# Two attention steps at a time: scores of four units, then values of four units, in every second step

## The reference

```python
s = jnp.einsum('znqhd,znkhd->znhqk', qb, kb) * (Dh ** -0.5)
s = jnp.where(valid[None, :, None], s + bias[None, None], -jnp.inf)
lse = jax.nn.logsumexp(s, axis=-1)
p = jnp.exp(s - lse[..., None])
o = jnp.einsum('znhqk,znkhd->znqhd', p, vb)
```

## Time and profile before

| | |
|---|---|
| median of three runs | 2827.86 us |
| profiled execution, own time | 2828.97 us |
| its span | 2827.2 us |
| TensorE busy | 2801.3 us, 99% |
| VectorE, ScalarE, GpSimd busy | 61%, 47%, 6% |
| granted TensorE clock, mean | 0.996 of 2.4 GHz |
| steps of the first attention (first score matmul to end of its filler) | 59.6 to 391.5 us |

### The profile page before, as it was taken

The page is one execution under the profiler, slowest core; times in us unless marked ns, Lnnn a source line. Parts: engine busy times, 40 slices in busy tenths (PEclk is TensorE's granted clock), DMA queues, the critical chain, the costliest instruction groups (busy, mean ns, idle before and its releaser), DMA issues.

```text
span 2827.2 us, 34929 instructions
## 1 busy us (share of the span) xinstructions
PE 2801.3 (99%) x13264; PEld 2270.1 (80%) x13264; DVE 1726.0 (61%) x2477; ACT 1333.7 (47%) x2149; POOL 180.7 (6%) x133
## 2 busy tenths in 40 slices
PE   8999999999999999999999999999999999999998
PEld 7777777888888888888777788888888888888886
DVE  5333356235866666678666524988235866666786
ACT  5444452114555454445355424887123655544452
POOL 1222420000000000000033200000000000000000
PEclk9999999999999999999999999999999999999998
DMA  3111111123344366532321111211113334384442
GB/s 127 38 31 38 39 38 51 52 62 117 131 149 153 150 236 231 186 109 93 128 61 53 45 54 59 60 54 59 53 60 142 134 149 156 139 322 162 156 134 71
DMA packets 86126, 302.75 MB, mean 107 GB/s; under 512 B 9552, under 2 KB 9680, under 8 KB 79696
## 3 DMA queue, kind: packets, MB, share of 16 engines
q1 hardware_dynamic: 84672, 295.88, 30.7%
q10 hardware_dynamic: 1296, 4.72, 0.6%
HBM read 225.07 MB, written 75.50 MB: 106 GB/s over the span
## 4 chain that ended last, share of the span: by engine, by line
PE 97%; DVE 1%; issue 1%; ACT 0%; DMA 0%; POOLq 0%; POOL 0%; SPq 0%; DVEq 0%; ACTq 0%
PE ps L404 24%; PE ps L2450 17%; PE pa L2756 11%; PE ps L2756 11%; PE ps L2785 9%; PE pa L2785 9%; PE pa L404 4%; PE ps L2803 3%; PE ps L2632 2%; PE pa L2560 2%; PE pa L2528 2%; PE pa L2539 1%; PE pa L2499 1%; PE pa L2632 0%; PE ps L2462 0%
## 5 line engine op out<-in xcount | busy, mean ns | idle before, releaser
L394 DVE TENSOR_TENSOR w_lo<-w_raw,w_hi 128x1024 fp32r<-128x1024 f32 x134 | 160.0, 1194 | 395.0 <-ACT w_hi L388 394.9
L388 ACT ACTIVATE w_hi<-w_raw 128x1024 fp32r<-128x1024 f32 x134 | 137.8, 1029 | 385.2 <-PE ps L404 265.7
L404 PE MATMUL ps<-a_hi,w_hi 128*128 128x512 f32 x896 | 276.5, 390 | 0.8 <-DVE a_lo L1756 0.8
L404 PE MATMUL ps<-a_hi,w_lo 128*128 128x512 f32 x896 | 275.9, 389 | 0.0
L404 PE MATMUL ps<-a_lo,w_hi 128*128 128x512 f32 x896 | 275.9, 389 | 0.0
L2450 PE MATMUL ps<-a_hi,w_hi 128*128 128x512 f32 x672 | 225.2, 416 | 9.2 <-DVE a_lo L1704 9.2
L1217 ACT ACTIVATE krh<-k_rraw 128x512 fp32r<-128x512 f32 x192 | 121.1, 631 | 229.8 <-PE ps L2785 118.0
L2450 PE MATMUL ps<-a_lo,w_hi 128*128 128x512 f32 x672 | 214.7, 401 | 0.0
L2450 PE MATMUL ps<-a_hi,w_lo 128*128 128x512 f32 x672 | 213.8, 399 | 0.0
L1984 DVE TENSOR_TENSOR krl<-k_rraw,krh 128x512 fp32r<-128x512 f32 x192 | 132.6, 691 | 132.3 <-ACT krh L1217 132.2
L404 PEld LDWEIGHTS ps<-a_hi,w_hi 128*128 128x128 f32 x896 | 167.7, 188 | 38.5 <-issue 2.5
(11 more groups left out here) (372 smaller groups left out, 6017.5 us busy)
## 6 DMA issues: line engine op xcount, KB each, us to landing
w_raw<-wstream SPq DMA_DIRECT2D x134, 512.0 KB, 3.5
k_rraw<-hff SPq DMA_DIRECT2D x224, 256.0 KB, 2.8
hff<-hbuf SPq DMA_DIRECT2D x32, 1024.0 KB, 3.9
wA<-wff SPq DMA_DIRECT2D x16, 2048.0 KB, 7.9
hff<-hbuf SPq DMA_DIRECT2D x32, 768.0 KB, 3.3
w_raw<-wff SPq DMA_DIRECT2D x32, 512.0 KB, 4.3
f_raw<-wff SPq DMA_DIRECT2D x32, 512.0 KB, 4.5
hres<-zt SPq DMA_DIRECT2D x16, 512.0 KB, 2.6
```

Source lines behind the costliest of these rows:

```text
L388: nc.scalar.activation(w_hi[:, slot, 0:n], w_raw[:, slot, 0:n], ACT.Copy).then_inc(s_whi, 1)
L394: nc.vector.tensor_tensor(w_lo[:, slot, 0:n], w_raw[:, slot, 0:n], w_hi[:, slot, 0:n].bitcast(F32), ALU.subtract).then_inc(s_wlo, 1)
L404: mm = nc.tensor.matmul(out[0:m, c], w[0:kp, slot, wofs:wofs + m], x[0:kp, k, c * HC:(c + 1) * HC], start=first and n == 0, stop=last and ...
```

## The change

In the first attention alone (b = 1) TensorE handles two steps together. In even steps it issues the scores of steps s and s+1 (four units), then the values of steps s-4 and s-3; odd steps have neither. The filler stays at 24 or 12 a step and now runs on over 52 steps, not 50, with the same total. Transposes stand one step later than before, units 2(s-2) and 2(s-2)+1 in step s. In odd steps the cuts of the filler are (0, 0, n/2, n): the first transpose stands at the head of the step, ahead of all filler, except where s mod 8 is 5. The scores of a second step go to columns 256 to 511 of the same two PSUM banks; VectorE waits with the first two units until both pairs are written. `pt` has four slots. ScalarE and VectorE take another order within a step: `unit_hi` and `unit_out` now stand first and `pool_hi` next, ahead of both evictions; evictions and exponentials alternate; `weights` and `operand_lo` stand ahead of `add_max`. The second attention keeps its order (`single_step`).

The new order of ScalarE, then of VectorE, then of TensorE:

```diff
-                for s in range(ns + 2):
+                def double_step(s):
                     p, q = divmod(s, STEPS_PER_PAIR)
-                    done = unit_at(b, s - 1) if s else None
+                    done = unit_at(1, s - 1) if s else None
+                    if p + 1 < npair and V_STEP[1] <= q < V_STEP[1] + VB[1]:
+                        v_out(VB[1] * (p + 1) + q - V_STEP[1])
+                    if done is not None:
+                        unit_hi(done)
+                        unit_out(done)
+                    if s in PHI_STEPS:
                         pool_hi(PHI_STEPS[s])
+                    for hh in range(2):
+                        if 2 <= s < ns + 2:
+                            probs_out(2 * (s - 2) + hh)
+                        if s < ns:
+                            exp(2 * s + hh)
+                        if hh == 0 and s >= 7 and (s - 7) % 4 == 0:
+                            o_out((s - 7) // 4)
+                    if scored_unit(1, s - 2):
+                        operand_hi(*scored_unit(1, s - 2))
...
+                def double_step(s):
+                    if s and unit_at(1, s - 1) is not None:
+                        weights(unit_at(1, s - 1))
+                    if s < ns:
+                        if scored_unit(1, s - 3):
+                            operand_lo(*scored_unit(1, s - 3))
+                        add_max(2 * s)
+                        add_max(2 * s + 1)
+                    if s + 1 in PHI_STEPS:
+                        pooled(PHI_STEPS[s + 1])
+                    if s in PLO_STEPS:
+                        pool_lo(PLO_STEPS[s])
...
+                def double_step(s, at):
                     p, q = divmod(s, STEPS_PER_PAIR)
+                    n = fill_of(1, s)
+                    if s % 2 == 0:
+                        for step in (s, s + 1):
+                            if s < ns:
+                                scores(2 * step)
+                        for step in (s - 4, s - 3):
+                            if s >= 4:
+                                values(2 * step)
+                    if p + 1 < npair and V_STEP[1] <= q < V_STEP[1] + VB[1]:
+                        pe.wait_ge(s_pt, 2 * (s - 2))
+                        v_batch(VB[1] * (p + 1) + q - V_STEP[1])
+                    cuts = (0, n // 3, 2 * n // 3, n) if s % 2 == 0 or q == V_STEP[1] + 1 else (0, 0, n // 2, n)
+                    for hh in range(2):
+                        fill(at + cuts[hh], at + cuts[hh + 1])
+                        if 2 <= s < ns + 2:
+                            transpose_probs(2 * (s - 2) + hh)
+                    fill(at + cuts[2], at + cuts[3])
+                    return at + n
```

The waits that change with it:

```diff
-                            if n == 0 and j >= 2:
+                            if n == 0 and j >= 2 and j % ahead == 0:
                                 pe.wait_ge(s_add, j + hh - 1)
...
-                    if j >= 2:
-                        act.wait_ge(s_pv, j - 1)
+                    if j >= slots:
+                        act.wait_ge(s_pv, j - slots + 1)
...
-                    dve.wait_ge(s_S, j + 1)
+                    dve.wait_ge(s_S, j + (3 if b == 1 and j % 4 < 2 else 1))
```

More of the change, by code:

```diff
@@ L769, in attention @@
                 nt = npair * UNITS_PER_PAIR
+                slots = 4 if b == 1 else 2
                 def unit_hi(m):
@@ L871, in probs_out @@
                     act.wait_ge(s_T, j + 1)
-                    if j >= 2:
-                        act.wait_ge(s_pv, j - 1)
-                    nc.scalar.activation(pt[:, j % 2, 0:w], pa[:, 2, 0:w], ACT.Copy).then_inc(s_pt, 1)
+                    if j >= slots:
+                        act.wait_ge(s_pv, j - slots + 1)
+                    nc.scalar.activation(pt[:, j % slots, 0:w], pa[:, 2, 0:w], ACT.Copy).then_inc(s_pt, 1)
                 def o_out(c):
@@ L915, in attention, with single_step @@
                 ns = npair * STEPS_PER_PAIR
-                for s in range(ns + 2):
+                def double_step(s):
                     p, q = divmod(s, STEPS_PER_PAIR)
-                    done = unit_at(b, s - 1) if s else None
-                    if b == 1 and s in PHI_STEPS:
-                        pool_hi(PHI_STEPS[s])
+                    done = unit_at(1, s - 1) if s else None
[5 more added lines that the diff above has]
+                    if s in PHI_STEPS:
+                        pool_hi(PHI_STEPS[s])
+                    for hh in range(2):
[7 more added lines that the diff above has]
+                        operand_hi(*scored_unit(1, s - 2))
+                def single_step(s):
+                    p, q = divmod(s, STEPS_PER_PAIR)
+                    done = unit_at(2, s - 1) if s else None
                     if s < ns:
                         exp(2 * s)
[L923 to L927, removed]
+                    if p + 1 < npair and V_STEP[2] <= q < V_STEP[2] + VB[2]:
+                        v_out(VB[2] * (p + 1) + q - V_STEP[2])
+                    if s < ns:
                         exp(2 * s + 1)
@@ L940, in attention @@
                         unit_out(done)
-                    if b == 2 and scored_unit(2, s - 1):
+                    if scored_unit(2, s - 1):
                         operand_hi(*scored_unit(2, s - 1))
-                    if b == 2 and p + 1 < npair and q in (1, 5, 7):
+                    if p + 1 < npair and q in (1, 5, 7):
                         load_bias(p + 1, (1, 5, 7).index(q))
-                    if b == 2 and s >= 10 and (s - 10) % 8 == 0:
+                    if s >= 10 and (s - 10) % 8 == 0:
                         a2_hi((s - 10) // 8)
+                for s in range(ns + (4 if b == 1 else 2)):
+                    if b == 1:
+                        double_step(s)
+                    else:
+                        single_step(s)
                 if b == 2:
@@ L1643, in attention @@
                         add_max(2 * s + 1)
[L1644 to L1655, removed]
-                        a2_lo((s - 11) // 8)
+                        if scored_unit(2, s - 2):
+                            operand_lo(*scored_unit(2, s - 2))
+                        normalise(2 * s)
+                        normalise(2 * s + 1)
+                    if s and unit_at(2, s - 1) is not None:
+                        weights(unit_at(2, s - 1))
+                    if s >= 11 and (s - 11) % 8 == 0:
+                        a2_lo((s - 11) // 8)
+                for s in range(ns + (4 if b == 1 else 2)):
+                    if b == 1:
+                        double_step(s)
+                    else:
+                        single_step(s)
                 if b == 2:
@@ L2434, in attention @@
                 batches = [0]
+                ahead = 4 if b == 1 else 2
                 def fill(m0, m1):
@@ L2520, in scores @@
                                 rhs = k[rows, (i + 1) * P - w:(i + 1) * P]
-                                out = pa[:, hh, 0:w]
+                                out = pa[:, hh, 256 * (i % 2):256 * (i % 2) + w]
                             else:
@@ L2561, in values @@
                                                   vtok[:, p % 2, blk, 64 * hh:64 * hh + 64],
-                                                  pt[:, hh, a * P:(a + 1) * P], start=(a == 0), stop=(a == nb - 1))
+                                                  pt[:, (j + hh) % ahead, a * P:(a + 1) * P], start=(a == 0), stop=(a == nb - 1))
                             if a == nb - 1:
@@ L2581, in attention, with single_step @@
                 at_fill = 48 * AHEAD
-                for s in range(ns + 2):
+                def double_step(s, at):
                     p, q = divmod(s, STEPS_PER_PAIR)
-                    third = fill_of(b, s) // 3
+                    n = fill_of(1, s)
+                    if s % 2 == 0:
+                        for step in (s, s + 1):
+                            if s < ns:
+                                scores(2 * step)
[12 more added lines that the diff above has]
+                    return at + n
+                def single_step(s, at):
+                    p, q = divmod(s, STEPS_PER_PAIR)
+                    third = fill_of(2, s) // 3
                     if s < ns:
@@ L2588, in attention @@
                         values(2 * (s - 2))
-                    if p + 1 < npair and V_STEP[b] <= q < V_STEP[b] + VB[b]:
+                    if p + 1 < npair and V_STEP[2] <= q < V_STEP[2] + VB[2]:
                         pe.wait_ge(s_pt, 2 * (s - 1))
-                        v_batch(VB[b] * (p + 1) + q - V_STEP[b])
+                        v_batch(VB[2] * (p + 1) + q - V_STEP[2])
                     for hh in range(2):
-                        fill(at_fill, at_fill + third)
-                        at_fill += third
+                        fill(at, at + third)
+                        at += third
                         if 1 <= s <= ns:
                             transpose_probs(2 * (s - 1) + hh)
-                    fill(at_fill, at_fill + third)
```

(5 more changed lines are left out.)

13 lines of the change are left out of this document (6 added, 7 removed).

## The result

The changed kernel takes 2833.22 us (median of 20 runs, 2830.70 to 2836.65), the kernel before 2827.90 in the same comparison. The ratio is 1.0020 with a 95% interval of 1.0015 to 1.0026: slower by 5.3 us, where 10.1 us less were forecast.

The account below looks back on a forecast made before the run. TensorE was taken as the bound, busy in all 332.00 us of the stage without a wait. -12.9 + 2.6 + 0.2 = -10.1 us against 2828.97 gave 2818.9; the median, 1.1 lower, 2817.8 us; range 2814.4 to 2821.8.

Parts of the forecast that it names:

- The saving of 24 blocks: TensorE, first attention: 24 of 50 score and value blocks appended to the block before, saving 12.9 us (12.4 to 13.4).
- pool_hi in steps 43 and 47: pool_hi ahead of both evictions on ScalarE stalls TensorE's transposes 1.3 us in each step, 2.6 us in all.
- 0 if `pooled` were early: Lower bound on the pool_hi stalls in steps 43 and 47: no stall if VectorE's pooled came early.
- Value transposes: Steps 5 and 13: a stall of 0 to 0.4 us each while awaiting an eviction, taken as 0.1, 0.2 for both.
- 0.3 or more: Slack claimed for the value transposes in the 128-wide pairs, in us.
- `operand_lo` 1.14 up to the next: VectorE's link in the chain ahead of the value transpose: operand_lo takes 1.14 us up to the next instruction.
- the same sum: Chain from the earlier value transpose's end to the eviction, 5.8 us with hand-overs, against TensorE's way of 5.85.
- The clock: Rival, 4%: TensorE's clock falls at the two new stalls, 2.7 us each, giving 2823.2 us.
- The rule cited in the forecast: TensorE idling briefly between groups again and again returns to half clock; by it both falls at the new stalls come.
- its own range: The main forecast's range, 2816.3 to 2819.6 us, from the saving, the stalls and the value transposes; forecast given 70%.
- the rival "slower": Rival, 4%: unit_hi and unit_out hold up every even step's first eviction, 20 steps; at 1 us over each, 2837.8 us.
- the estimate of 4.6 us for narrow matmuls: Within the 2% rival of faster narrow matmuls: 152 appended pairs at the skill's 81 ns would save 4.6 us.

Follow-up runs that it names:

- VectorE's old order: Changed kernel with VectorE's add_max, add_max, operand_lo, weights as before, and ScalarE's pool_hi between the two evictions: 2814.14 us, ratio 0.9950.
- GpSimd out of the way: Changed kernel, VectorE and ScalarE left as changed, with GpSimd starting a scaling only when operand_lo of the unit before is done: 2817.83 us, ratio 0.9964.
- the single steps with the collision: Kernel before, TensorE unchanged, with ScalarE's unit_out right behind unit_hi and VectorE's operand_lo right behind weights: 2835.86 us, ratio 1.0025.

## Why the prediction was wrong, step by step

The sum was -12.9 + 2.6 + 0.2 = -10.1 us. The stage of the profiled executions went from 332.2 to 339.2, +7.0. Its terms as measured:

- **The saving of 24 blocks: right.** Forecast 12.9 (12.4 to 13.4). With `operand_lo` behind `add_max` the stage is 10.5 us shorter than before, and two waits stand in it, of 1.39 us each by the distances between starts; 10.5 + 2.8 = 13.3. The kernel with VectorE's old order gives 332.2 - 319.8 = 12.4 and 0.8 of wait, 13.2.
- **pool_hi in steps 43 and 47: right.** Forecast 1.3 each, measured 1.39. Its bound below "0 if `pooled` were early" was no real one, but what takes its place was not seen: `weights` held by GpSimd.
- **Value transposes: the step that failed.** Forecast 0.1 each at two places and "0.3 or more" of slack at the other three; measured, by distances between starts, 2.1 to 2.6 us at all five, 11.8 in all. The chain was followed rightly, and with GpSimd out of the way it holds: a weight load waits 0.15 us at each of the two places and at none of the other three. Wrong was the term "`operand_lo` 1.14 up to the next": it was read from a row in which GpSimd was idle, and I moved it next to GpSimd's scaling without asking what GpSimd then does. I asked of GpSimd only whether its window sums come in time, not what it runs beside. The row gave the length of a neighbourhood, not of the instruction. At 3.4 to 3.9 us the same sum gives 5.8 + 2.2 to 2.7 against 5.85: a stall of 2.2 to 2.7.
- **The clock: priced, and given 4%.** The rival had falls at the stalls of 1.3 us, at 2.7 us each. Those caused none. Behind three of the five longer stands (2.60, 2.35 and 2.38 us) the clock fell, each time for 3.4 us by the trace, and each cost about 1.6 us: eight fillers at 0.427 and not 0.231. That is 4.8 us. The rule cited in the forecast from the Trainium skill (TensorE: Matmul & The Clock Gate, section "A second HAM failure mode: psum-queue depth-cycling") is of a TensorE that idles briefly between groups, and often. The long stands lie some 60 us apart, so it isn't shown that the falls are of the kind that this rule means; falls there are behind three of five stands of 2.1 us and more, and none behind the 1.4 us ones. Which of the long ones they strike isn't told by their length: the stand of 2.37 us had none, and the first one, of 2.1 us, had none here but one in the execution with `pool_hi` last.
- Against the kernel with `operand_lo` behind `add_max` the stage is 17.4 us longer; 11.8 and 4.8 leave 0.8, which lies in short delays of some 0.12 us between the stands and was not in the sum. Some 0.55 of it is the same collision once more, in the double steps behind the stands, where the keys' `operand_lo` is held: in step 8 it runs from 105.04 to 108.46, and `add_max` behind it, the exponential (109.28) and the eviction behind that (109.78) come late, so that the transpose at the head of step 9 starts at 110.25, 0.56 behind the fillers before it and not 0.46. Another 0.16 follows a `weights` that GpSimd holds for 2.06 us (354.29).

Together -13.3 + 2.8 + 11.8 + 4.8 + 0.8 = +6.9, against +7.0. The sum closes by its making, since the saving and the 0.8 are both read against the kernel with `operand_lo` behind `add_max`; the saving of 13.2 with VectorE's old order, the 2.8, the 11.8 and the 4.8 are read apart from each other. The whole runs differ by 5.3. The profiled executions differ by 5.2 in span: the changed one began the stage 0.9 later, and had shorter stretches at half clock at the start of the second attention (1.6 less) and at the end of the program (1.0 less). The window that answers to the earlier trace rows, moved by the 6 to 8 us by which it comes later:

```profile
1365.00:1375.00 10.00, 10.00 (x47) 8.24 (x47) 5.11 (x11) 1.37 (x3) 1.64 (x1) 0.83 0.01 2
```

0.83 and not 0.73: 3.4 us at half clock and not 5.4 or more. The kernel with `operand_lo` behind `add_max` had none there and one near 437 us, and the single steps with the collision had some 3.4 us there as well, so the shorter fall doesn't need the merged steps. What sets it isn't shown.

Smaller slips in the prediction change nothing here: its own range comes out of its terms as 2816.5 to 2819.9 and not 2816.3 to 2819.6; the 18.5 us of the rival "slower" are 15.8 counted from 2817.8; and the estimate of 4.6 us for narrow matmuls takes each pair as one matmul of 128 columns, where a pair is two and 48 of the 72 score pairs have 256.

Of the rivals, "slower" was right in its sign and wrong in its place: it had ScalarE's copies hold up the first eviction of every even step, where VectorE's `operand_lo` held up the second in five. The Trainium skill has the rule that speaks against this change and that the forecast lacked: SBUF — State Buffer, section "Who interferes with whom", says that a VectorE instruction with two inputs in SBUF contends with a GpSimd instruction that reads SBUF, and that one of them then waits for the whole of the other. The runs here agree: 3.93 us is 2.84 us of waiting for GpSimd's end and 1.09 of work, while `add_max`, with one of its inputs in PSUM, isn't slowed. In the other direction the runs show little: GpSimd's scaling takes 3.03 us at 149.17, where it starts 0.28 us before the end of VectorE's `weights` (148.22 to 149.45), and 2.92 at 153.32 in the kernel before, beside nothing but `add_max`. That is 0.11 more, where by that rule it would be blocked for the 0.28; spans of GpSimd are rough in the profile.

## What to carry to other kernels

Merging like matmuls was worth what distances between starts had said, to 0.4 us in 13: those can be trusted for the engine that is moved. A duration from a row holds only as long as the instruction keeps its neighbours on the other engines: when an elementwise operation of VectorE with two inputs in SBUF is moved, or what releases GpSimd is moved, look at what GpSimd runs at the new place, and price the operation at its own length plus the rest of GpSimd's. And where one stall on a chain is removed, follow the next instruction of the same queue before counting the gain.

## What the runs showed of the hardware

- GpSimd holds up VectorE on 128x1024 elementwise work with two inputs out of SBUF for the whole rest of its own instruction, and not by some per cent: 1.22 us becomes 3.4 to 3.9, and all ten `operand_lo` of the changed kernel end 1.07 to 1.10 us after GpSimd's instruction does. No common tile is needed: `weights` (2.80 us for 1.23) shares none with the window sums. The add (one input in PSUM) and the maximum (one input) kept their 0.41 and 0.42 us beside the same GpSimd operation.
- A stand of TensorE of 2.1 to 2.6 us, by starts, can bring the clock down to 1.2 GHz for 3.4 us: three times in five in one execution, twice in five in the execution with `pool_hi` last, never in five of 1.5 to 2.0 us (the collision in the kernel before). A stand of 2.4 us so costs up to 4 us. The middle half of the changed kernel's runs spreads over 3.5 us (2832.2 to 2835.8), against 1.2 before (2827.4 to 2828.6); that the falls make this spread is likely, but not shown.
